# Order of VectorE's work in layer 1's grouped-query rounds: copies first, maximum last

## What is computed

```python
def attend_gqa(q, k, v):
    s = jnp.einsum('bqhgd,bkhd->bhgqk', q, k).astype(jnp.float32) * HEAD_SCALE
    p = jax.nn.softmax(s, axis=-1).astype(v.dtype)
    return jnp.einsum('bhgqk,bkhd->bqhgd', p, v)

def odd_mixer(...):
    ...
    o_lat = merge(sweep_query_blocks(lambda a: attend_gqa(a, gk_all, gv_all), gq),
                  neighbourhood_attention(nq, nk, nv, nk_c, nv_c, na_rpb))
```

## Time and profile before

| | |
|---|---|
| median of 3 runs | 1753.72 us (1753.65 to 1753.98) |
| the profiled execution | 1753.11 us |
| its span, first to last instruction | 1751.3 us |
| TensorE busy | 1661.1 us, 95% |
| VectorE busy | 1084.0 us, 62% |
| ScalarE busy | 674.4 us, 39% |
| GpSimd busy | 169.9 us, 10% |
| mean granted TensorE clock | 0.990 of full speed |

### The profile page before, as it was taken

How to read it: one execution, slowest core, us unless ns; L and a number is a source line. 1 busy time by engine, 2 the same in 40 slices (tenths; PEclk the granted TensorE clock), 3 DMA queues, 4 the chain that set the end, 5 groups by cost and what they waited for, 6 DMA issues and landing times.

```text
span 1751.3 us, 27075 instructions
## 1 busy us (share of the span) xinstructions
PE 1661.1 (95%) x10508; PEld 1471.6 (84%) x10508; DVE 1084.0 (62%) x1908; ACT 674.4 (39%) x1291; POOL 169.9 (10%) x214
## 2 busy tenths in 40 slices
PE   5899999988989999999999999999999899999997
PEld 3899888777979899899899878997778788888885
DVE  2779788675375756756756778725684744444446
ACT  3434366654373122122122146325674532222221
POOL 3000166231000000000000000002341000000000
PEclk9999999999999999999999999999999999999999
DMA  9342521013102423423423312203023122222221
GB/s 362 115 147 97 154 64 37 11 58 121 49 25 73 168 105 113 161 105 118 152 107 124 128 65 97 73 1 97 1 73 121 49 97 97 96 96 96 96 96 48
DMA packets 30261, 170.40 MB, mean 97 GB/s; under 512 B 3921, under 2 KB 6865, under 8 KB 12113
## 3 DMA queue, kind: packets, MB, share of 16 engines
q1 hardware_dynamic: 30160, 169.03, 27.3%
HBM read 156.17 MB, written 2.10 MB: 90 GB/s over the span
## 4 chain that ended last, share of the span: by engine, by line
PE 83%; DVE 7%; issue 4%; ACT 3%; DMA 2%; POOL 1%; SPq 0%; DVEq 0%; ACTq 0%
PE ps L1134 24%; PE ps L888 14%; PE ps L890 14%; PE ps L889 14%; PE ps L955 3%; PE ps L1070 2%; PE ps L969 2%; PE ps L1045 2%; PE ps L989 1%; PE ps L984 1%; DVE nmax L2420 1%; PE ps L1033 1%; PE ps L1023 1%; DVE wlo L1947 1%; DVE h L2091 1%
## 5 line engine op out<-in xcount | busy, mean ns | idle before, releaser
L1427 ACT ACTIVATE whi<-raw 128x2048 fp32r<-128x2048 f32 x86 | 164.2, 1910 | 302.5 <-PE ps L890 281.9
L1947 DVE TENSOR_TENSOR wlo<-raw,whi 128x2048 fp32r<-128x2048 f32 x86 | 197.0, 2290 | 123.4 <-ACT whi L1427 123.1
L888 PE MATMUL ps<-whi,uhi 128*128 128x512 f32 x640 | 250.0, 391 | 0.6 <-DVE wlo L1947 0.6
L890 PE MATMUL ps<-whi,ulo 128*128 128x512 f32 x640 | 249.1, 389 | 0.0
L889 PE MATMUL ps<-wlo,uhi 128*128 128x512 f32 x640 | 249.1, 389 | 0.0
L1134 PE MATMUL ps<-ahi,whi 128*128 128x384 f32 (+1 forms) x720 | 215.3, 353 | 1.1 <-ACT relu L1806 1.1
L1134 PE MATMUL ps<-alo,whi 128*128 128x384 f32 (+1 forms) x720 | 215.2, 353 | 0.0
L1134 PE MATMUL ps<-ahi,wlo 128*128 128x384 f32 (+1 forms) x720 | 215.2, 352 | 0.0
L2355 DVE SCALAR_TENSOR_TENSOR ada_junk<-raw,silu_rows 128x1024 bf16<-128x1024 f32 x160 | 195.5, 1222 | 26.3 <-DMA raw<-in_w_ada_t 23.7
L888 PE MATMUL ps<-whi,ahi 128*128 128x256 f32 x592 | 171.2, 289 | 10.0 <-DVE alo L2052 4.9
L889 PE MATMUL ps<-wlo,ahi 128*128 128x256 f32 x592 | 169.0, 286 | 0.0
(11 more groups left out here) (255 smaller groups left out, 3066.3 us busy)
## 6 DMA issues: line engine op xcount, KB each, us to landing
raw<-in_w_ff SPq DMA_DIRECT2D x64, 1024.0 KB, 4.8
raw<-in_w_ada_t SPq DMA_DIRECT2D x40, 1024.0 KB, 4.8
raw<-in_w_in_odd SPq DMA_DIRECT2D x9, 1024.0 KB, 4.9
raw<-in_w_in_even SPq DMA_DIRECT2D x8, 1024.0 KB, 4.9
first_raw<-in_w_ada SPq DMA_DIRECT2D x6, 1024.0 KB, 15.8
h<-in_x SPq DMA_DIRECT2D x4, 1024.0 KB, 7.8
raw<-in_w_out_even SPq DMA_DIRECT2D x4, 1024.0 KB, 6.8
raw<-in_na_bias SPq DMA_DIRECT2D x4, 1024.0 KB, 6.3
```

The source lines that it names most:

```text
L888: pe.matmul(dst, lhs[0], rhs[0], start=first, stop=False)
L890: return pe.matmul(dst, lhs[1], rhs[0], start=False, stop=last)
L1427: act.activation(whi[w % 2][:, :, :], raw[r % 2][:, :, :], ACT.Copy).then_inc(s_hi, 1)
L1947: dve.tensor_tensor(wlo[w % 2][:, :, :], raw[r % 2][:, :, :], whi[w % 2][:, :, :].bitcast(F32), ALU.subtract).then_inc(s_lo, 1)
```

## The change

In VectorE's loop, `maxima(i)` of the grouped-query rounds moves from ahead of `inverses(i - 1)` and `probs_a(i - 3)` to behind both. In the neighbourhood rounds it stays where it was. Nothing else is changed; the instructions are the same.

```diff
                 for i in range(N_ODD + 5):
-                    if i < N_ODD:
+                    if i >= N_GQA and i < N_ODD:
                         maxima(i)
                     if 1 <= i <= N_ODD:
                         inverses(i - 1)
                     if 3 <= i < N_ODD + 3:
                         probs_a(i - 3)
+                    if i < N_GQA:
+                        maxima(i)
                     if 5 <= i and (i - 5 >= N_GQA or i % 2 == 0):
                         output_lo(odd_value_of(i - 5))
```

## The result

The changed kernel has a median of 1759.71 us in 7 runs (1755.72 to 1761.57), against 1753.98 us in 7 runs of the kernel before (1752.36 to 1755.6). The ratio is 1.0031, with a 95% interval of 1.0021 to 1.0041: slower by 5.4 us, 3.7 to 7.2 by the interval. The profiled execution has a span of 1756.1 us.

What follows compares the result with a forecast made beforehand. VectorE and ScalarE taking turns were to outlast TensorE's grouped-query pace, 5.10 us a pair against 4.82; 3.7 start-up plus 3.8 for 27 rounds, less 2.0 given back, made 5.5, so 1753.72 + 5.5 = 1759.2 us, range 1756.6 to 1762.0.

Steps and rivals of the forecast that it cites:

- the sum: Grouped-query stage: starts added round by round put the first neighbourhood scores 5.50 us later, giving 1759.2 us.
- The four links: VectorE and ScalarE, each round: maximum to exponential 0.99, to inverse 1.02 to 1.03, to copy 0.07 to 0.08, to maximum 0.46.
- The other rings: Grouped-query stage: shorter wait cycles through scores, transposes and copy, 4.14 and 4.53 us a pair of rounds, not deciding.
- the new ring: Exponential i-1, inverse i-1, copy i-3, maximum i, exponential i in turn: 2.55 us a round, 5.10 a pair against 4.82.
- Start and end: Stage edges: maximum 29 is 7.5 us late, 2.0 given back by scores 32, leaving 5.50 us.
- the start-up: First grouped-query rounds: the engine's two rounds in hand are lost, 3.7 us of the shift at maximum 29.
- Nothing won back behind: Neighbourhood rounds onward: TensorE sets the pace, so the 5.5 us go through; layer-boundary clock at most 1.7 us either way.
- Rival (a), the gain: Grouped-query stage: early copy alone counts, 0.29 us less a pair, 3.8 us in 13 pairs, 1749.9 us; chance 0.02.
- Rival (b), the start-up alone: Grouped-query stage: ring at or below 2.41 us a round, only start-up lost, 1.7 us later, 1755.4 us; chance 0.05.
- Rival (c), full durations behind a wait: VectorE: instruction ends don't overlap behind a wait, 2.75 us a round, 1764.6 us; chance 0.04.
- Rival (d), the clock: Start of stage: longer TensorE holes drop the clock to 1.2 GHz for two or three pairs, 1767 to 1770 us; chance 0.03.
- a clock below 1.00 in the stage: Grouped-query stage: a granted TensorE clock below 1.00 was listed as showing the prediction wrong.

Runs made afterwards that it cites:

- the kernel with the copy first: Copy, maximum, inverse order in rounds 0 to 31, against the kernel before: median 1750.48 us, ratio 0.9977.
- even rounds only: Inverse, copy, maximum order only in even grouped-query rounds, odd rounds as before, against the kernel before: median 1751.05 us, ratio 0.9977.
- the third profile: Changed kernel run a third time, nothing else altered, against the kernel before: 1760.86 us in one run, stage 78.25 us, no low clock.
- the first profile: Changed kernel as first measured, against the kernel before: median 1759.71 us, ratio 1.0031, stage 79.12 us, clock low once.
- the second: Changed kernel profiled again, nothing else altered, against the kernel before: median 1760.58 us, ratio 1.0035, stage 79.09 us, clock low once.

## Why the prediction was right

The time was forecast as 1759.2 us, 5.5 above before; the median is 5.7 above it, and the ratio gives 5.4. The mechanism is the forecast one. That the times meet within 0.2 us is partly luck: the interval is 3.7 to 7.2 us, and two of three profiles hold 0.84 us of a low clock that the sum leaves out. By its steps:

- **The four links.** Maximum to exponential was 0.99 in the sum and is 0.98; exponential to inverse 1.02 to 1.03, and 1.03; inverse to copy 0.07 to 0.08, and 0.08; copy to maximum 0.46, and 0.45. The round is 2.54 to 2.56 where 2.55 was taken, and in the steady state, from maximum 3 at 1198.99 on, 26 rounds take 66.52 us to maximum 29 at 1265.51, 2.558 each. The rows that counted were those of the first rounds, where each engine had waited for the other; in the steady pair most of these links are covered by a queue.
- **The other rings.** At 4.14 and 4.53 a pair they were not to decide while the new ring was there. The 4.53 comes into its own once the ring is open: 4.56 in the kernel with the copy first, 4.56 with even rounds only (maxima at 1223.73 and 1228.29). This was a number of the prediction that nothing in the changed kernel could test.
- **Start and end.** The shift at the first neighbourhood scores was forecast as 5.50 us. Without the low clock it is 5.67 (the third profile), with it 6.5. In the first profile it shows as 1270.55 against 1265.51, only 5.04, because the program came to the stage 1.50 us earlier. The parts hold one by one: 7.68 us late at maximum 29 for 7.5, of which the start-up is 3.7 for 3.7 and the rounds 4.0 for 3.8, and 2.01 given back for 2.0. The distance from scores 32 to scores 33, left out of the sum as 0.19 us more, is 2.10 for 1.87 before.
- **Nothing won back behind.** 485.6 to 486.3 us follow the stage in the three profiles of the changed kernel, 485.8 before. This was right, and the allowance of 1.7 us for the clock at the layer boundary was more than what appeared.
- **Rival (a), the gain.** It has the right mechanism with a false condition. The 0.29 us a pair are real and were won by two kernels, 3.2 and 3.7 us in the stage against the 3.8 at most of the prediction. The change as written couldn't have them, because the inverse and the copy moved together.
- **Rival (b), the start-up alone.** Falls by the distance of 2.54 to 2.56 us between maxima, where it needed 2.41.
- **Rival (c), full durations behind a wait.** Falls too: the copy starts 0.08 us after an inverse of 0.16 that had waited, and the next maximum 0.45 after a copy of 0.54. The sentence of the Trainium skill that it went with ("VectorE: DVE Perf Modes", section "The DRAIN you can't avoid") is not borne out for these operations. The same section adds that a next operation that is not held starts earlier; the prediction left that out, and the starts here agree with it.
- **Rival (d), the clock.** Its mechanism occurred and its price was too high. I priced two or three pairs at half speed, 7 us or more. In fact one set of scores and transposes was slow in the first profile and two in the second, TensorE has slack while the ring decides, and only 0.84 us came through in either. The prediction called a clock below 1.00 in the stage a sign of its being wrong; over the stretch of the earlier trace rows it was 0.98 in the first profile and 0.95 in the second, and this sign was too strict. The prediction gave this rival 0.03; the clock itself fell in two of the three profiles.

In the stage the measured loss is above the sum, by 0.2 us, or by 1.0 with the low clock. The time before the stage moved by up to 1.7 us from the first profile before, either way, which is more than both.

## What to carry to other kernels

In a hand-written queue, ask of every instruction that is moved which wait it is moved behind, and follow that wait until it comes back to the same instruction: if it does, the sum of the starts around the ring is a lower bound on the pace, however idle each engine looks. Split a reordering into its moves and price each by itself; here the copy's move alone is 0.23% faster (0.9967 to 0.9987), the inverse's alone can't be told from no change, and the two together are 0.31% slower. Read the links of a new ring from the first rounds of a loop, where the engines wait for one another, and don't guess the duration of an operation from its size if another engine can be in the same memory at the time.

## What the runs showed of the hardware

- A VectorE product of two SBUF inputs (128x256) took 0.88 us beside a GpSimd scaling that had started first and 0.42 us without it, and ended 0.26 us after GpSimd. It looks held until the other is done rather than slowed. Where the product started first it took 0.41 us, and the scaling 1.00 instead of 0.91. The Trainium skill, "SBUF — State Buffer", section "SBUF: two separate sides", says this: of a VectorE operation with two SBUF inputs and a GpSimd operation that reads SBUF, the one that starts first has the shared pair of ports for the whole instruction, and the other waits. The trace agrees. The copies out of PSUM keep 0.54 to 0.56 us beside the same scaling.
- The record of a VectorE operation ends a little after the next one can start, also when the first had itself waited: a copy of 0.56 us that had waited 1.48 is followed after 0.47, a maximum of 0.96 that had waited 1.79 after 0.87, and an inverse of 0.16 that had waited 1.06 after 0.08.
- TensorE's granted clock fell (mean 0.64 over 1194 to 1198 us) after holes of 1.38 and 1.12 us ahead of two sets of scores, and didn't in five profiles with the same or longer holes at a later time. Before, the first of these holes is there and the clock stays at 1.00. The Trainium skill, "TensorE: Matmul & The Clock Gate", section "Part 1: The HAM clock gate (the "warmup" mystery)", calls the interval in which activity is watched free-running; the dependence on when the stage begins would fit that, but no run here moved it on purpose.
